# Three output chunks in column halves, and the norm of the context tokens moved under gate chunks

## The reference: what is computed

```
h_lat = h_lat + gate_l * out_l          # out = mixed @ w_out of layer 0, 1024 x 1024
h_ctx = h_ctx + gate_c * out_c
xl = rms_norm(h_lat) * (1 + scale_l) + shift_l     # layer 1
xc = rms_norm(h_ctx) * (1 + scale_c) + shift_c
cq, ckv, kr, z = split(x @ w_in)        # cq 256, ckv 128, kr 64, z 1024 columns
q  = rms_norm(cq) @ wq_b ;  kv = rms_norm(ckv) @ wkv_b
o  = attention(q, k, v);  out_l = (o * silu(z)) @ w_out
```

## Time and profile before

| | |
|---|---|
| median of 3 runs | 1149.93 us (1145.72 to 1150.44) |
| profiled execution, its own time | 1151.13 us |
| its span, first to last instruction | 1149.2 us |
| mean granted TensorE clock | 0.976 |
| costliest line group | L1830 pj<-h_hi,w_hi, 1472 matmuls, 460.0 us |
| next two | L1831 445.9 us, L1832 445.7 us |
| share of PE in the chain that ended last | 82% (DVE 8%, ACT 5%) |

### The profile page before, as it was taken

The page is one execution under the profiler, slowest core; times in us unless marked ns, Lnnn a source line. Parts: engine busy times, 40 slices in busy tenths (PEclk is TensorE's granted clock), DMA queues, the critical chain, the costliest instruction groups (busy, mean ns, idle before and its releaser), DMA issues.

```text
span 1149.2 us, 20599 instructions
## 1 busy us (share of the span) xinstructions
PE 1091.5 (95%) x7991; PEld 964.6 (84%) x7991; DVE 734.7 (64%) x1559; ACT 628.3 (55%) x1279; POOL 2.6 (0%) x10
## 2 busy tenths in 40 slices
PE   5889999988978899999999999999999999999997
PEld 3667777766867677999899999999989999999997
DVE  4422476567555566778878767557688686656664
ACT  3253334476337654647766775445467666664443
POOL 0000000000000000000000000000000000000000
PEclk8899999999988999999999999999999999999998
DMA  9987553111312421645554565666464555556652
GB/s 313 278 241 220 183 166 92 55 46 47 110 46 65 113 62 56 170 117 149 142 146 130 147 166 165 184 184 183 111 166 129 147 147 147 147 160 186 182 171 74
DMA packets 264872, 165.04 MB, mean 144 GB/s; under 512 B 7092, under 2 KB 262824, under 8 KB 264776
## 3 DMA queue, kind: packets, MB, share of 16 engines
q1 hardware_dynamic: 264384, 163.02, 49.5%
q0 software_dynamic: 192, 0.66, 0.2%
q10 hardware_dynamic: 200, 0.06, 0.0%
HBM read 162.66 MB, written 1.05 MB: 142 GB/s over the span
## 4 chain that ended last, share of the span: by engine, by line
PE 82%; DVE 8%; ACT 5%; issue 3%; SPq 1%; DMA 1%; DVEq 0%; ACTq 0%
PE pj L1830 23%; PE pj L1831 21%; PE pj L1832 21%; DVE w_lo L1219 2%; ACT w_hi L762 1%; PE tr L2276 1%; PE ac L2112 1%; PE sc L2100 1%; PE ac L2216 1%; PE tr L2011 1%; PE sc L2004 1%; PE pj L1917 1%; PE ac L2025 1%; PE sc L2198 1%; PE sc L2196 1%
## 5 line engine op out<-in xcount | busy, mean ns | idle before, releaser
L1830 PE MATMUL pj<-h_hi,w_hi 128*128 128x256 f32 (+1 forms) x1472 | 460.0, 313 | 13.2 <-DVE w_lo L1219 5.3
L1831 PE MATMUL pj<-h_lo,w_hi 128*128 128x256 f32 (+1 forms) x1472 | 445.9, 303 | 0.0
L1832 PE MATMUL pj<-h_hi,w_lo 128*128 128x256 f32 (+1 forms) x1472 | 445.7, 303 | 0.0
L1219 DVE TENSOR_TENSOR w_lo<-raw,w_hi 128x1024 fp32r<-128x1024 f32 (+1 forms) x258 | 309.3, 1202 | 184.4 <-ACT w_hi L762 183.7
L1830 PEld LDWEIGHTS pj<-h_hi,w_hi 128*128 128x128 f32 x1472 | 283.3, 192 | 46.6 <-issue 25.0
L762 ACT ACTIVATE w_hi<-raw 128x1024 fp32r<-128x1024 f32 (+1 forms) x258 | 267.5, 1039 | 56.9 <-PE pj L1832 56.9
L1832 PEld LDWEIGHTS pj<-h_hi,w_lo 128*128 128x128 f32 x1472 | 283.6, 193 | 10.7
L1831 PEld LDWEIGHTS pj<-h_lo,w_hi 128*128 128x128 f32 x1472 | 284.0, 193 | 10.2 <-issue 1.2
L1830 PE MATMUL pj<-m_hi,w_hi 128*128 128x256 f32 (+1 forms) x352 | 110.1, 313 | 10.1 <-DVE w_lo L1219 6.0
L1831 PE MATMUL pj<-m_lo,w_hi 128*128 128x256 f32 (+1 forms) x352 | 109.1, 310 | 0.0
L1832 PE MATMUL pj<-m_hi,w_lo 128*128 128x256 f32 (+1 forms) x352 | 108.9, 309 | 0.0
(11 more groups left out here) (308 smaller groups left out, 1321.3 us busy)
## 6 DMA issues: line engine op xcount, KB each, us to landing
raw<-in_w_in_dram SPq DMA_DIRECT2D x152, 512.0 KB, 3.8
ada_raw<-in_ada_w_dram SPq DMA_DIRECT2D x48, 512.0 KB, 6.9
raw<-in_even_w_in_dram SPq DMA_DIRECT2D x28, 512.0 KB, 4.9
raw<-in_w_branch_dram SPq DMA_DIRECT2D x24, 512.0 KB, 3.4
raw<-in_w_out_dram SPq DMA_DIRECT2D x16, 512.0 KB, 4.0
raw<-in_odd_w_in_dram SPq DMA_DIRECT2D x11, 512.0 KB, 4.1
raw<-in_even_w_out_dram SPq DMA_DIRECT2D x8, 512.0 KB, 3.7
raw<-in_odd_w_out_dram SPq DMA_DIRECT2D x8, 512.0 KB, 3.8
```

Of the source, the lines that this page charges most:

```text
L1219: last = nc.vector.tensor_tensor(lo, src, hi.bitcast(F32), ALU.subtract)
L1830: nc.tensor.matmul(dst, lh, rh, start=first, stop=False)
L1831: nc.tensor.matmul(dst, lh, rl, start=False, stop=False)
L1832: return nc.tensor.matmul(dst, ll, rh, start=False, stop=final)
```

## The change

**The last three eout chunks** (5, 6, 7; `HALVED` = 5) are multiplied twice over 256 columns: first the latent halves of all three, each into its own bank, then the context halves into three banks that lie idle there (`ctx_bank`: the second `sc` bank and both `tr` banks). The latent sums and 1/sqrt column are made while PE does context halves. The split of cq0, cq1 and cz0 waits for the context half that frees the weight buffer.

**The context norm** gets a column and rows of its own: PE sums in the middle of cz0, DVE makes the column, PE spreads it at three quarters of cz1, and the eight context tiles are normed in slots 3, 4 and 5 (`L1_NORM`).

**Order of layer 1**: the four gate chunks cz0 to cz3 stand before ckv and kr, and wq0 before wkv0. cq0 and cq1 are interleaved tile by tile. `L1_FREE` is the index of wkv0 plus 1, so it goes from 7 to 10: up to there ACT and DVE split weights first in a slot.

**The small norms** use columns instead of rows: PE sums to a column (4 one-column matmuls), DVE's `column_rsqrt` of 12 small operations, PE spreads it (`latent_spread`) inside the kr chunk. Ln, Exp and the full-row Newton step go.

**Second block**: the three parts of `h_norm` move one slot later, each behind the slot's `split_lo`.

```diff
-    l1 = [("cq", 0), ("cq", 1), ("ckv", 0), ("kr", 0), ("cz", 0), ("cz", 1),
-          ("wkv", 0), ("wq", 0), ("cz", 2), ("wq", 1), ("wkv", 1), ("wq", 2), ("cz", 3), ("wq", 3)]
+    l1 = [("cq", 0), ("cq", 1), ("cz", 0), ("cz", 1), ("cz", 2), ("cz", 3), ("ckv", 0), ("kr", 0),
+          ("wq", 0), ("wkv", 0), ("wq", 1), ("wkv", 1), ("wq", 2), ("wq", 3)]
-CQ_STAT, KV_STAT = 2, 3
+CQ_STAT = 4
+HALVED = 5
+LAT_SLOT = L1_CHUNKS.index(("kr", 0))
+L1_NORM = {3: (KT, KT + 2), 4: (KT + 2, KT + 5), 5: (KT + 5, 2 * KT + 1)}
-NORM_SLOT = {0: (0, 1, 2), 1: (3, 4, 5), 2: (6, 7)}
+NORM_SLOT = {1: (0, 1, 2), 2: (3, 4, 5), 3: (6, 7)}
...
# weights_used
+            if L0_IN + HALVED <= before < L0_IN + KT:
+                eng.wait_ge(ctx_done, before - L0_IN - HALVED + 1)
...
# ACT, between the layers (squares of chunks 5 to 7 are latent only)
-            split_hi(C0 + AHEAD)
+            split_hi(C0)
+            context_square(HALVED)
+            split_hi(C0 + 1)
+            context_square(HALVED + 1)
             act.wait_ge(amod_set, 10)
...
+            l1_norm_hi(0, KT - 2)
+            split_hi(C0 + 2)
+            l1_norm_hi(KT - 2, KT)
+            context_square(HALVED + 2)
...
# DVE, between the layers
-            norm_rsqrt(1, 4)
-            modulated_norm(1, 0, 2 * KT)
+            norm_rsqrt(1, 2)
+            context_residual(HALVED)
+            split_lo(C0)
+            context_residual(HALVED + 1)
+            dve.wait_ge(rs_set, 2)
+            l1_tmp(0)
+            l1_tmp(1)
+            split_lo(C0 + 1)
+            for v in range(2, KT):
+                l1_lo(v - 2)
+                l1_tmp(v)
+            l1_lo(KT - 2)
+            l1_lo(KT - 1)
+            split_lo(C0 + 2)
+            context_residual(HALVED + 2)
...
# DVE, slots of layer 1
+                if 1 <= s < L1_FREE:
+                    split_lo(C0 + s + AHEAD)
+                if s == 2:
+                    context_rsqrt()
+                if s == 3:
+                    dve.wait_ge(ctx_rs, 1)
+                if s in L1_NORM:
+                    l1_norm(*L1_NORM[s])
+                if s == LAT_SLOT:
+                    dve.wait_ge(lat_rs, 1)
...
+                    latent_rsqrt(kv_stat, kv_sums, C_KV_RANK, 2)
...
+                if s == CQ_STAT + 2:
+                    latent_rsqrt(q_stat, q_sums, C_Q_RANK, 1)
...
# DVE, second block
-                dve.wait_ge(rs_set, 3 + lay)
-                h_norm(0, 3)
...
                     if s == 1:
+                        dve.wait_ge(rs_set, 3 + lay)
+                        h_norm(0, 3)
+                    if s == 2:
                         h_norm(3, 6)
-                    if s == 2:
+                    if s == 3:
                         h_norm(6, KT + 1)
...
# PE, between the layers
-            sum_squares(1, 4)
-            spread(1, 4)
+            for m in range(HALVED, KT):
+                g = G1_OF[("eout", m)]
+                pe.wait_ge(lo_done, L0_IN + m + 1)
+                group_bank_free(pe, g, None)
+                half_project(m, LAT, bank(g)[:, LAT]).then_inc(proj_done, 1)
+            pe.wait_ge(tr_free, TR1_OF[("p1", 0)])
+            for m in range(HALVED, KT):
+                half_project(m, CTX, ctx_bank[m - HALVED]).then_inc(ctx_done, 1)
+                if m == HALVED:
+                    sum_squares(1, 2)
+                elif m == HALVED + 1:
+                    spread(1, 2)
+            pe.wait_ge(ctx_sq, 2)
+            for n, src in enumerate((rs_t, scr[:, HALVED % 2, :], scr[:, (HALVED + 1) % 2, :])):
+                for i in range(2):
+                    last = nc.tensor.matmul(ctx_sums[:, i:i + 1], src[:, SEQ + P * i:SEQ + P * i + P], ones[:, 0:1],
+                                            start=(n == 0 and i == 0), stop=False)
...
# PE, slots of layer 1
+                    if s == 0:
+                        for k in range(KT):
+                            for c in range(2):
+                                project(C0 + c, moving=(n_lo, lambda j: 2 * KT + j + 1), part=(k / KT, (k + 1) / KT))
+                    elif s == LAT_SLOT:
+                        project(C0 + s, part=(0.0, 0.25))
+                        latent_spread(sc[:, 1, :], q_stat, 2, 1)
+                        pe.wait_ge(lat_sq, 3)
+                        for i in range(4):
+                            last = nc.tensor.matmul(kv_sums[:, i:i + 1], scr[:, 0, P * i:P * i + P], ones[:, 0:1], start=(i == 0),
+                                                    stop=(i == 3))
+                        last.then_inc(lat_mm, 1)
+                        project(C0 + s, part=(0.25, 0.875))
+                        latent_spread(sc[:, 0, :], kv_stat, 4, 2)
+                        project(C0 + s, part=(0.875, 1.0))
+                    elif s == 2:
+                        project(C0 + s, part=(0.0, 0.5))
+                        pe.wait_ge(ctx_sq, 3)
...
+                    elif s == 3:
+                        project(C0 + s, part=(0.0, 0.75))
+                        pe.wait_ge(ctx_col, 1)
...
```

More of the change, by code:

```diff
@@ L1025, in _ @@
             for s in range(L1_IN + L1_DRAIN):
+                if s == LAT_SLOT + 1:
+                    act.wait_ge(lat_tmp, 3)
+                    nc.scalar.activation(kvn_hi, ntmp[:, 0:2, :].rearrange("p a n -> p (a n)"), ACT.Copy).then_inc(lat_hi, 1)
                 if 1 <= s < L1_FREE:
@@ L1374, in modulated_norm @@
                     u = 2 * KT * layer + v
-                    if layer == 1 and v == KT + 1:
-                        split_lo(C0 + AHEAD)
                     if v < v1:
@@ new lines, in l1_tmp, with l1_lo @@
+            def l1_tmp(v):
+                k, half = norm_tile(1, v)
+                cols, rows = ((LAT, sc[:, 0, LAT]), (CTX, ctx_rows))[half]
+                u = 2 * KT + v
+                nc.vector.scalar_tensor_tensor(ntmp[:, u % 4, :], x_t[:, k, cols], amod[:, 1, half, k:k + 1], rows,
+                                               ALU.mult, ALU.mult).then_inc(n_tmp, 1)
+            def l1_lo(v):
+                k, half = norm_tile(1, v)
+                norm_lo(2 * KT + v, k, (LAT, CTX)[half], mod[:, 1, k, half:half + 1])
@@ new lines, in _, with latent_rsqrt, context_rsqrt @@
+            l1_lo(KT - 2)
+            l1_lo(KT - 1)
+            split_lo(C0 + 2)
+            context_residual(HALVED + 2)
+            def latent_rsqrt(stat, sums, count, done):
+                dve.wait_ge(lat_mm, done)
+                after(nc.vector.tensor_scalar(stat[:, 0, :], sums, 1.0 / count, NORM_EPS, ALU.mult, ALU.add))
+                column_rsqrt(stat[:, 2, :], stat[:, 0, :], stat[:, 1, :]).then_inc(lat_col, 1)
+            def context_rsqrt():
+                dve.wait_ge(ctx_mm, 1)
+                after(nc.vector.tensor_scalar(col[:, 0, 2:4], ctx_sums, 1.0 / D, NORM_EPS, ALU.mult, ALU.add))
+                column_rsqrt(col[:, 2, 2:4], col[:, 0, 2:4], col[:, 1, 2:4]).then_inc(ctx_col, 1)
@@ L2118, in l1_turn, with latent_spread @@
                     turn_probs(TR1_OF[("p1", u)], (prob_set, 16 + u + 1), prob[:, u % 2, :], TOK)
+            def latent_spread(dst, stat, nt, value):
+                pe.wait_ge(lat_col, value)
+                for i in range(nt):
+                    last = nc.tensor.matmul(dst[:, P * i:P * i + P], stat[:, 2, i:i + 1].broadcast_to([P, P]), ident,
+                                            start=True, stop=True)
+                last.then_inc(lat_rs, 1)
             def out_part(tiles, a, b):
@@ L2155, in _ @@
+                if s == CQ_STAT:
+                    pe.wait_ge(lat_sq, 2)
+                    for i in range(4):
+                        last = nc.tensor.matmul(q_sums[:, i % 2:i % 2 + 1], scr[:, i // 2, P * (i % 2):P * (i % 2) + P],
+                                                ones[:, 0:1], start=(i == 0), stop=(i == 3))
+                    last.then_inc(lat_mm, 1)
                 if s - 1 in L1_PAIR:
```

139 lines of the change are left out of this document (74 added, 65 removed).

## The result

The changed kernel takes 1140.34 us (median; 1138.70 to 1141.88) where the kernel before, run beside it on the same chip, takes 1148.60. The ratio is 0.993, with a 95% interval of 0.9903 to 0.9958. In a second comparison (experiment 5) it was 1139.75 against 1149.90, ratio 0.9911 (0.9889 to 0.9934). So it is faster by 8 to 10 us; forecast were 11.8 us less, and 1138.1.

A forecast was written before the change was run, and what follows sets the result against it. PE, busy 95% of the span, bounds the kernel; only its waits and low clock can give time. -9.2 - 2.6 + 0.3 - 0.3 = -11.8 us from 1151.13, less 1.2 to the median, gives 1138.1 us; range 1133 to 1145.

The forecast's parts named there:

- stalls add up: Rival: stalls add up on ACT and DVE, hand-overs in a row from 328 to 368 us; gain only 6 to 9 us; chance 0.20.
- the forecast's band: The main case for the whole kernel: a gain of 9 to 15 us; chance 0.62.
- more: Rival: waits between cq1 and wkv0 vanish, the second block's go in part; -17.7 us, 1132.2 us; chance 0.06.
- A: Third-last eout chunk to end of cq1: halves hide the norm's column; 25.9 us against 35.1, -9.2 us.
- B: End of cq1 to wkv0's first matmul: new order removes waits and low clock; -2.6 us, bounds -6.9 and +2.
- The four waits: PE waits before wkv0: context column in cz1 1.35, q column in kr 0.7, kr's bank 0.8, wq0's bank 1.5 us.
- the four table loads: ACT's table loads that go; said to lie in the old waits before wkv0 and not counted again.
- C: wkv0 to end of wq3: low clock -2, scores +0.9, wkv1 +1.4; +0.3 us, bounds -2 and +4.
- D: Second block: four weight waits go, but the norm comes late; -0.15 a layer, -0.3 us; bounds -3.9 and +2.
- No change: Rival: the gain comes back at wkv0 and wkv1 as bank waits, +8 us; -3.8 us, 1146 us; chance 0.07.
- Slower, the clock: Rival: repeated short PE waits keep the clock low, costing 29.6 us; 1167.7 us; chance 0.05.

The follow-up runs named there:

- experiment 5: The changed kernel once more, unaltered, beside three later variants on the same chip: 1139.75 us, ratio 0.9911 to the kernel before.
- Experiment 4: Changed kernel with all three context halves ahead of the latent sums of squares, so nothing lies under the norm's column: 1145.92 us, ratio 0.9969.
- Experiment 6: Changed kernel with L1_FREE one lower (9), so ACT takes out wq0's groups before it splits wkv1's weights: 1139.05 us, ratio 0.9909.
- experiment 7: Changed kernel with two of DVE's columns earlier: the context's ahead of its slot's weight split, q's one slot earlier: 1139.69 us, ratio 0.9914.
- experiment 3: Kernel before with only the new chunk order, latent statistics in cz2 and kr, kvn tile one slot earlier; no halves, old norms: 1153.54 us, ratio 1.0037.
- experiment 1: Kernel before with only the second block's norm tiles moved one slot later, behind the weight splits: 1150.74 against 1149.49 us, ratio 1.001.
- experiment 11: Changed kernel with only cz0 and cz1 ahead of ckv, cz2 and cz3 back between the wkv and wq chunks: 1141.27 us, ratio 0.9923.

## Why the prediction was right, point by point

- **The time**: 1140.34 lies in the range of 1133 to 1145, 2.2 us above the forecast. By the time alone the first comparison does not separate the forecast from the rival "stalls add up": its gain of 8.3 us is in that rival's band (6 to 9), and 1140.34 is nearer to its 1141.3. The second comparison, 10.2 us, is in the forecast's band. The stretches decide. (The low end of the range was not "half way to more", which is 1135, but 1133.)
- **What bounds the kernel**: right. The removed idle time and the low clock behind it are the gain.
- **A, -9.2**: -9.31. The latent half, the sums and the column ran as placed (column 325.29 to 327.62 on DVE; the context half of chunk 6 ends at 328.06, and the spread follows with no wait). cq1 ends at 25.82 us (25.9 said), but not for the reason given. DVE came to its first `h_lo` 0.5 us sooner than planned, PE's own sums held cq0 back until 19.84 us (19.8 said), and from there PE went mostly at its own pace of 0.72 a tile and met DVE only from tile 6 on, for under 0.1 us at a time: 19.84 + 8 x 0.72 = 25.6. The two paths lay within 0.3 us of each other, so the sum came out either way; that it did is partly luck. Experiment 4 shows what gives A: the cover. Without it the halves' smaller latent norm leaves 1.8 us.
- **B, -2.6**: -2.5. The four waits were 1.06, 0.64, 0.74 and 1.52 (said: 1.35, 0.7, 0.8, 1.5), together 3.96 against 4.35. ckv found its context tiles ready. Experiment 6 confirms the cause of the 1.52, experiment 7 that of the first two (it removes both). That the four table loads had to go for the order not to cost more than it gives, the plan did not say (experiment 3).
- **C, +0.3**: +0.9, the sum's second largest miss. The low clock of wkv0 gave 1.64 (384.09 - 376.92 before against 377.75 - 372.22 after), 2 was said. Scores +0.89 (0.9 said). wkv1 waits 1.36, but it had waited 0.48 already, so +0.88 where +1.4 was said. In a slot between two pairs 8.17 us pass in place of 7.74, +0.43, with a wait of 0.27 for the probabilities that I had not seen. That is +0.6. The other 0.4 is what PE needs to start a stream of another kind, which the plan left out: in the timelines 0.16 more at pair 0's scores, 0.19 at wq1 behind them, and 0.07 and 0.12 in two groups of scores, less 0.15 elsewhere.
- **D, -0.3**: +1.0, wrong in sign: the step of the sum that failed. On PE it held in the first layer: the first scores of the first layer come 31.39 us behind the layer's sums, 31.56 before, -0.17 for the -0.15 said. What failed is "a layer" as the end of it. The next thing that PE needs, the rotated `x_t`, is DVE's, and DVE's row of work had moved back with the norm tiles: the scores on `x_t` start 39.81 us behind the sums, 39.63 before, with a wait of 0.89 in place of 0.55. I had followed the tiles to q0 and not what stood behind them on DVE, which is the very thing that a moved step asks for. The plan worked out the first layer and took it twice; in the second the wait for `h_lo` is 1.82 us in place of 1.37, and without low clock (experiment 1) it is +0.28 at the first scores and +0.62 at `x_t`. And the sum left out that 1.04 and 0.91 rolled into one 1.82 can turn the clock down: +1.20 at the first scores of the changed kernel's second layer, of which the shorter wait for `x_t` (0.23) takes 0.3 back. The clock is the smaller part: it makes +0.86 out of +0.62. My list of idle times with low clock behind them (2.5, 1.8, 3.4, 3.2) could not warn of it: the kernel before is at 0.50 already from 334 us, in the wait of 2.5, so the 1.8 behind it did not turn the clock down.
- **The rivals**: the profile's 9.8 us lie 2.0 short of the forecast; D is 1.3 of that and C 0.6. Not "stalls add up" as it was meant, on DVE and ACT in A (A and B came to 0.1 us), though what is short in C is stalls at wkv; not "more" (the waits of B stood, until experiments 6 and 7 took them out). "No change" had the stalls at wkv in kind (2.3 us in sight), not eight us of them. "Slower, the clock": 1.00 in every window up to wkv0.
- The distance to the median: 0.8 us of the profile's 10.6 are the start.

## What to carry to other kernels

Cover a norm's reduction with matmuls that don't need it (7.5 of 9.3 us at the end of cq1, experiment 4), and put its small operations on the engine that need not load tables. A new order can cost when what stood between two chunks had covered an evacuation (experiment 3); the cover with the old order was not run. When a step is moved, follow what stands behind it on its engine to the next thing that TensorE needs: two waits of 1.04 and 0.91 against one of 1.82 looked like a gain and cost 0.6 us without the clock and 0.9 to 1.4 with it. Read small edits by stretches between marks of the trace that repeat to 0.1 us, not by medians that a start of varying length moves by 2.

## What the runs showed of the hardware

Whether the clock falls behind a single wait is not certain. Seven profiles (of six kernels) have the norm tiles behind all the splits. Behind the wait of 1.82 us at the head of the second layer the granted clock fell in six of the seven (in the changed kernel to 0.51 and 0.64 in two windows of 2 us), and behind the wait of 1.37 at the head of the first layer in one of seven. In six profiles with one or two waits of 0.9 to 1.4 for `w_lo` in the same places it fell in none of twelve layers. In experiment 11 it fell at 0.47 and 1.21 us of waiting with 0.9 us of matmuls between them, within ckv, with 512-column matmuls. But in experiment 3 it stayed at 1.00 behind a wait of 2.20 us before cz1, longer than all of these, and in the changed kernel behind 0.74 and 1.52 us, 1 us of matmuls apart. So what decides is not the length of the last wait alone, and what else does is open. The Trainium skill, "TensorE: Matmul & The Clock Gate", section "A second HAM failure mode: psum-queue depth-cycling", describes a kernel in which short idle spells between groups of matmuls, often repeated, swing the clock. Experiment 11 agrees in kind, with two short spells and one fall (0.60 and 0.55 in two windows), where the prediction had found no such case.
